# SSD chunk states of a hybrid decoder trunk: from two fp32 products in the block of y to six fp32r products inside the next projection unit

## What is computed

```python
def step(h, inp):                      # one chunk of 128 tokens
    xc, dtc, bc, cc = inp
    cum = jnp.cumsum(dtc * a, axis=1)
    ...
    y = jnp.einsum('btsg,btsgh,bsghp->btghp', scores, decay, xdt)
    y = y + jnp.einsum('btgn,bghpn->btghp', cc, h) * jnp.exp(cum)[..., None]
    last = cum[:, -1]
    w_end = jnp.exp(last[:, None] - cum)
    h_new = h * jnp.exp(last)[..., None, None] + jnp.einsum('bsgn,bsgh,bsghp->bghpn', bc, w_end, xdt)
    return h_new, y
```

## Time and profile before

| what | value |
|---|---|
| median of 3 runs | 950.2 us (949.51 to 950.45) |
| the profiled execution's own time | 950.12 us |
| its span, first to last instruction | 947.5 us |
| PE busy | 936.0 us (99%), mean granted clock 0.999 |
| DVE busy | 683.9 us (72%) |
| ACT busy | 426.2 us (45%) |
| POOL busy | 43.5 us (5%) |
| DMA | 112.54 MB, mean 119 GB/s |

### The profile page before, as it was taken

One profiled execution on the slowest core, in us unless ns is written; L12 is line 12 of the kernel. 1 busy time (PEld: TensorE's weight loads), 2 busy tenths in 40 slices (PEclk: granted clock), 3 DMA queues, 4 the chain that ended last, 5 costly groups with the idle time before them and its releaser, 6 DMA issues.

```text
span 947.5 us, 18763 instructions
## 1 busy us (share of the span) xinstructions
PE 936.0 (99%) x7928; PEld 890.6 (94%) x7928; DVE 683.9 (72%) x934; ACT 426.2 (45%) x714; POOL 43.5 (5%) x148
## 2 busy tenths in 40 slices
PE   9999999999999999999999999999999999999996
PEld 7999999999989889999999999999999988999996
DVE  6897778766986569674558877778689757786544
ACT  6432553325774145533343225532377643555243
POOL 0000101110010000000000001111101000000000
PEclk9999999999999999999999999999999999999999
DMA  7334212144335463423432342122423451652222
GB/s 279 106 125 134 69 67 67 53 127 141 109 90 174 139 230 126 141 80 114 133 128 72 131 145 68 46 68 69 161 90 122 134 194 61 225 204 73 87 71 100
DMA packets 38420, 112.54 MB, mean 119 GB/s; under 512 B 11104, under 2 KB 14048, under 8 KB 36928
## 3 DMA queue, kind: packets, MB, share of 16 engines
q1 hardware_dynamic: 37936, 109.87, 35.5%
q0 software_dynamic: 256, 0.88, 0.3%
q10 hardware_dynamic: 144, 0.59, 0.2%
HBM read 93.85 MB, written 17.47 MB: 118 GB/s over the span
## 4 chain that ended last, share of the span: by engine, by line
PE 90%; DVE 4%; ACT 4%; issue 1%; DMA 0%; SPq 0%; DVEq 0%; ACTq 0%
PE acc L564 26%; PE acc L566 25%; PE acc L565 25%; PE misc L709 1%; ACT decay L1054 1%; PE misc L695 1%; PE misc L762 1%; ACT w_hi L962 1%; PE misc L784 1%; DVE w_lo L1250 1%; PE acc L854 1%; PE misc L803 1%; PE misc L834 1%; ACT decay L1061 1%; PE misc L726 1%; DVE conv_out L1613 1%
## 5 line engine op out<-in xcount | busy, mean ns | idle before, releaser
L564 PE MATMUL acc<-hin,w_hi 128*128 128x288 f32 x1504 | 450.9, 300 | 0.3 <-DVE x L1698 0.3
L566 PE MATMUL acc<-hin,w_lo 128*128 128x288 f32 x1504 | 442.9, 295 | 0.0
L565 PE MATMUL acc<-hin,w_hi 128*128 128x288 f32 x1504 | 442.9, 294 | 0.0
L564 PEld LDWEIGHTS acc<-hin,w_hi 128*128 128x128 f32 x1504 | 282.1, 188 | 13.0 <-issue 11.3
L962 ACT ACTIVATE w_hi<-w_raw 128x1024 fp32r<-128x1024 f32 x119 | 125.7, 1056 | 366.4 <-PE acc L566 365.8
L565 PEld LDWEIGHTS acc<-hin,w_hi 128*128 128x128 f32 x1504 | 282.3, 188 | 0.4
L566 PEld LDWEIGHTS acc<-hin,w_lo 128*128 128x128 f32 x1504 | 282.1, 188 | 0.0
L1250 DVE TENSOR_TENSOR w_lo<-w_raw,w_hi 128x1024 fp32r<-128x1024 f32 x119 | 145.4, 1222 | 118.7 <-ACT w_hi L962 118.3
L564 PE MATMUL acc<-mix,w_hi 128*128 128x288 f32 x416 | 123.4, 297 | 0.7 <-DVE vT L1277 0.4
L566 PE MATMUL acc<-mix,w_lo 128*128 128x288 f32 x416 | 122.5, 295 | 0.0
L565 PE MATMUL acc<-mix,w_hi 128*128 128x288 f32 x416 | 122.5, 294 | 0.0
(11 more groups left out here) (226 smaller groups left out, 1053.5 us busy)
## 6 DMA issues: line engine op xcount, KB each, us to landing
w_raw<-in_w SPq DMA_DIRECT2D x119, 512.0 KB, 3.6
decay<-cum_rows SPq DMA_DIRECT2D x8, 1024.0 KB, 7.1
h<-in_ssm SPq DMA_DIRECT2D x16, 512.0 KB, 6.2
out_ssm_s<-h SPq DMA_DIRECT2D x16, 512.0 KB, 6.0
x<-in_x SPq DMA_DIRECT2D x7, 576.0 KB, 7.1
x_kept<-x SPq DMA_DIRECT2D x4, 576.0 KB, 3.0
x<-x_kept SPq DMA_DIRECT2D x4, 576.0 KB, 6.1
out_y<-x SPq DMA_DIRECT2D x8, 288.0 KB, 2.4
```

The costliest lines, as they stand in the source:

```text
L564: pe.matmul(out, wh, hi, start=k == 0, stop=False)
L565: pe.matmul(out, wh, lo, start=False, stop=False)
L566: return pe.matmul(out, wl, hi, start=False, stop=k == KT - 1)
```

## The change

It makes these edits:

- The two fp32 state sums leave `ssd_y`. A new `ssd_states(t)` makes six fp32r products of 512 columns (for each group high B by high `xdw`, high B by low `xdw`, low B by high `xdw`). It is called inside `project` of the next even unit, 28 + 2t, behind its fifth step of sixteen, and waits for `s_xlo`.
- ACT writes the copy of B as fp32r (the high part). After reading an even unit's result it waits for `s_xdt` and copies `xdw` to fp32r, 128x1024 (signals `s_xhi`).
- DVE subtracts for the low part of B (128x256, ahead of `ssd_weights`) and for the low part of `xdw` (128x1024, a new `ssd_low`, behind `ssd_weights` and ahead of `pool`; it waits for `s_xhi`, signals `s_xlo`, and writes over `xdw`).
- `ssd_2` keeps the multiplication of the state (now signalled as `s_elu`, for which ACT's `el` waits in place of `s_h`) and the additions of y. The addition of the sum moves to a new `ssd_state`, at the end of DVE's odd turn, behind `c_decay`; it signals `s_h`.
- In unit 34 `pool_mm_` runs as the second insert, behind step 8, as before.

`ssd_turn` is not edited: it still waits for `s_h` and `s_y`.

```diff
+        xdw_lo = place("xdt_to_end_low", [P, HEADS * HD], F32R, at=work + 4 * 7168)
+        xdw_hi = place("xdt_to_end_high", [P, HEADS * HD], F32R, at=two_at)
+        btok_2 = place("b_tok_high_low", [P, 2, GROUPS * P], F32R, at=masked)
@@ PE
+            def ssd_states(t):
+
+                pe.wait_ge(*of(s_xlo, t + 1))
+                for g in range(GROUPS):
+                    b, c = slice(g * P, (g + 1) * P), slice(g * 512, (g + 1) * 512)
+                    pe.matmul(mb[:, g, :], btok_2[:, 0, b], xdw_hi[:, c], start=True, stop=False)
+                    pe.matmul(mb[:, g, :], btok_2[:, 0, b], xdw_lo[:, c], start=False, stop=False)
+                    mm = pe.matmul(mb[:, g, :], btok_2[:, 1, b], xdw_hi[:, c], start=False, stop=True)
+                mm.then_inc(s_S, 1)
+
             def ssd_y(t):
                 n = rows(t)
                 pe.wait_ge(*of(s_xdt, t + 1))
                 pe.wait_ge(*of(s_bt, t + 1))
-                if t < TILES - 1:
-                    for g in range(GROUPS):
-                        mm = pe.matmul(mb[:, g, :], btok[:, g, :], xdw[:, g * 512:(g + 1) * 512], start=True, stop=True)
-                    mm.then_inc(s_S, 1)
                 pe.wait_ge(*of(s_M, t + 1))
@@
-                    elif U_GPOOL < u < U_GPOOL + 4 and (u - S_SSD) % 2 == 0:
-                        project(u, lambda: pool_mm_(u - U_GPOOL - 1))
+                    elif S_SSD < u < S_SST and (u - S_SSD) % 2 == 0:
+                        sums = functools.partial(ssd_states, (u - S_SSD) // 2 - 1)
+                        if U_GPOOL < u < U_GPOOL + 4:
+                            project(u, sums, 4, functools.partial(pool_mm_, u - U_GPOOL - 1), KT - 1)
+                        else:
+                            project(u, sums, 4)
@@ ACT
                     if t > 1:
-                        eng.wait_ge(*of(s_h, t))
+                        eng.wait_ge(*of(s_elu, t - 1))
                     go(act(el[:, :], m[:, :, CH - 1], ACT.Exp), s_row, t)
@@
-                        go(act(btok[:, :, :], mb[:, 3, 0:256].rearrange("p (g n) -> p g n", g=2), ACT.Copy),
-                           s_bt, t + 1)
+                        if t < TILES - 1:
+                            go(act(btok_2[:, 0, :], mb[:, 3, 0:256], ACT.Copy), s_bt, t + 1)
+                        else:
+                            go(act(btok[:, :, :], mb[:, 3, 0:256].rearrange("p (g n) -> p g n", g=2), ACT.Copy),
+                               s_bt, t + 1)
@@
+                    if even and t < TILES - 1:
+                        eng.wait_ge(*of(s_xdt, t + 1))
+                        go(act(xdw_hi[:, :], xdw[:, :], ACT.Copy), s_xhi, t + 1)
@@ DVE
+            def ssd_low(t):
+
+                eng.wait_ge(*of(s_xhi, t + 1))
+                settle()
+                go(V.tensor_tensor(xdw_lo[:, :], xdw[:, :], xdw_hi[:, :].bitcast(F32), ALU.subtract), s_xlo, t + 1)
+
             def ssd_weights(t):
                 n = rows(t)
+                if t < TILES - 1:
+                    eng.wait_ge(*of(s_bt, t + 1))
+                    go(V.tensor_tensor(btok_2[:, 1, :], mb[:, 3, 0:256], btok_2[:, 0, :].bitcast(F32), ALU.subtract))
                 eng.wait_ge(*of(s_exp, t + 1))
@@
+            def ssd_state(t):
+
+                eng.wait_ge(*of(s_S, t + 1))
+                st = mb[:, 0:2, :].rearrange("p a n -> p (a n)")
+                if t == 0:
+                    eng.wait_ge(*of(rp_out, 32))
+                settle()
+                if t == 0:
+                    go(V.tensor_copy(hT[:, :], st), s_h, 1)
+                else:
+                    go(V.tensor_tensor(hT[:, :], hT[:, :], st, ALU.add), s_h, t + 1)
+
             def ssd_2(t):
                 n = rows(t)
-                if t < TILES - 1:
-                    eng.wait_ge(*of(s_S, t + 1))
...
-                        go(V.tensor_tensor(hT[:, :], hT[:, :], st, ALU.add), s_h, t + 1)
-                    settle()
-                eng.wait_ge(*of(s_Y, t + 1))
+                eng.wait_ge(*of(s_Y, t + 1))
+                if 0 < t < TILES - 1:
+                    settle()
+                    go(V.tensor_tensor(heads(hT[:, :]), heads(hT[:, :]),
+                                       el[:, :].unsqueeze(2).to_broadcast([P, HEADS, HD]), ALU.mult), s_elu, t)
+                settle()
                 for j in range(PAIRS):
@@
                         (ssd_weights if even else ssd_2)(t)
+                        if even and t < TILES - 1:
+                            ssd_low(t)
                         if (u - S_SSD) % 2 == 1 and t + 1 < TILES - 1:
                             c_decay(t + 1)
+                        if not even and t < TILES - 1:
+                            ssd_state(t)
```

More of the change, by code:

```diff
@@ L2 @@
 from contextlib import ExitStack
+import functools
 import numpy as np
@@ L319, in trunk @@
         s_bt = sem("ssd_b_tok", TILES)
+        s_elu = sem("ssd_decay_used", TILES - 2)
+        s_xhi = sem("ssd_to_end_high", TILES - 1)
+        s_xlo = sem("ssd_to_end_split", TILES - 1)
         s_exp = sem("ssd_exps", TILES)
@@ L1433, in c_decay @@
                         go(ins, s_ec, t)
+            def ssd_state(t):
[8 more added lines that the diff above has]
+                    go(V.tensor_tensor(hT[:, :], hT[:, :], st, ALU.add), s_h, t + 1)
             def ssd_2(t):
                 n = rows(t)
-                if t < TILES - 1:
-                    eng.wait_ge(*of(s_S, t + 1))
-                    st = mb[:, 0:2, :].rearrange("p a n -> p (a n)")
-                    if t == 0:
-                        eng.wait_ge(*of(rp_out, 32))
-                        settle()
-                        go(V.tensor_copy(hT[:, :], st), s_h, 1)
-                    else:
-                        eng.wait_ge(*of(s_Y, t + 1))
[L1446 to L1449, removed]
-                        go(V.tensor_tensor(hT[:, :], hT[:, :], st, ALU.add), s_h, t + 1)
+                eng.wait_ge(*of(s_Y, t + 1))
+                if 0 < t < TILES - 1:
                     settle()
-                eng.wait_ge(*of(s_Y, t + 1))
+                    go(V.tensor_tensor(heads(hT[:, :]), heads(hT[:, :]),
+                                       el[:, :].unsqueeze(2).to_broadcast([P, HEADS, HD]), ALU.mult), s_elu, t)
+                settle()
                 for j in range(PAIRS):
```

## The result

The changed kernel takes 965.42 us (median of 4 runs, 963.59 to 966.45) against 950.12 us before: a ratio of 1.0162, 95% interval 1.015 to 1.0174. It is slower by 15.3 us, and stays inside the range of 958.5 to 967. The profiled execution took 963.59 us, with a span of 961.7.

What follows compares the result with a forecast made beforehand. PE, busy 99%, was taken as the bound. Per layer, waits of 8.20 us less 0.20 and 1.84 of work gave +6.16, +12.3 in all: 950.12 to 962.4 us, range 958.5 to 967.

Steps and rivals of the forecast that it cites:

- The bound and the mechanism: PE's issued work sets the time; with s_h last in DVE's odd turn, PE's next turn must wait for it.
- The sum: Per layer: waits 8.20, less 0.20, less 1.84 of PE work, giving +6.16; +12.3 in all, 962.4 us.
- DVE's chain in chunk 1: Units 28, 29: low part of xdw from 241.65, state multiplication at 248.38, addition done 255.55, PE's turn at 255.63.
- y's waits: PE waits for s_M before y, no longer covered by the state sum: 0.52, 0.67, 0.54 us in chunks 0 to 2.
- chunk 3: Units 32 to 34: no new waits; pooling product 0.20 earlier, products save 0.46, shift +6.16.
- The price of the products: Six fp32r products of 512 columns take 1.35 us in place of 1.81, saving PE 0.46 a chunk.
- The turn's waits: PE waits for DVE's state addition at the turns after chunks 1 and 2: 3.09 and 3.38 us.
- Rival 3: PE's clock falls in each layer's two long waits, about 2.1 us a fall: 966.6 or 970.8 us; chance 0.08.
- my signs of being wrong: Turns of units 30 and 32 start without wait, six products cost 1.8 or more, or granted clock leaves 1.00 there.
- SP: State store and four loads, waiting for chunk 3's s_h, start about 0.8 us later against PE; hidden.
- Rival 1: The change does what its work count says and is faster: -4.0 us, about 946.2; chance 0.03.
- Rival 2: Only y's waits appear, because DVE hides more: -0.6 us, 949.5, no measurable change; chance 0.03.

Runs made afterwards that it cites:

- run 1: The changed kernel with DVE's addition of the state ahead of c_decay instead of behind it: 954.4 us, ratio 1.0047 against the kernel before.
- run 3: The kernel before, fp32 sums kept in the block of y, with only the state's addition moved behind y's additions and c_decay: 955.81 us, ratio 1.0067.
- Run 4: The changed kernel with 18 idle fp32r products of 288 columns on PE ahead of the turns of units 30 and 32: 962.02 us, ratio 1.0128.
- run 9: The kernel of run 5 with DVE's low part of xdw moved behind the pooling group: 947.41 us, ratio 0.9976 against the kernel before.
- run 5: The changed kernel with the addition ahead of c_decay, pooling groups moved to unit 30 and turn 34, and s_M signalled in halves: 947.95 us, ratio 0.9981.
- run 2: The changed kernel with the fourth pooling group (5.1 us of DVE) moved from unit 30 to unit 32: 967.38 us, ratio 1.0197.
- run 6: The changed kernel with only the pooling groups moved, third to unit 30, fourth to turn 34 behind the second gate: 957.8 us, ratio 1.0084.
- run 7: The changed kernel with only s_M signalled in halves, for each group of heads: 967.23 us, ratio 1.0181.
- run 8: The changed kernel with the sums behind the unit's ninth step instead of the fifth (pooling product behind the tenth): 967.14 us, ratio 1.018.

## Why the prediction was right, point by point

**The bound and the mechanism: right.** "The change makes `s_h` the last thing of that turn" is what runs 1 and 3 show from both sides.

**The sum: right to 0.2 us a layer, without the clock.** I had +6.16 a layer. Run 4, where the clock stayed up, has 86.31 - 79.99 = +6.32 (86.31 is the mean of its two layers). Its 962.02 us stand beside the forecast of 962.4. DVE's chain in chunk 1 came within 0.1 us from the low part of `xdw` on: multiplication 248.38 forecast, 248.36 measured; turn 255.63 and 255.66. PE's own errors, on y's waits and on the products, are larger than that. They leave the sum alone in chunks 1 and 2, because DVE sets the turn there and PE's wait takes up the difference. In chunk 3 two errors offset each other, which is luck: the pooling product came 0.31 nearer to the product before it, not 0.20, and the six products saved 0.32 and not 0.46 (21.55 - 22.19 = -0.64 in run 4, beside -0.66).

**The price of the products: the saving was mis-sized.** Six products took 1.35 in my sum. The timeline of PE after:

```profile
226.84 0.40 PE L701 MATMUL misc<-xdt_to_end_high,b_tok_high_low 128*128 128x512 f32 x1
227.07 0.39 PE L702 MATMUL misc<-xdt_to_end_low,b_tok_high_low 128*128 128x512 f32 x1
...
227.99 0.39 PE L703 MATMUL misc<-xdt_to_end_high,b_tok_high_low 128*128 128x512 f32 x1
228.22 0.29 PE L571 MATMUL acc<-hin,w_hi 128*128 128x288 f32 x1
```

228.22 - 226.84 = 1.38, and 1.40 in six of the eight chunks: at the upper end that I had from the width. By the Trainium skill ("TensorE: Matmul & The Clock Gate", Back-to-back issue gap), which gives its formula for a single product's gap and not for a stream with weight loads, the estimate was 1.30 for six; the measurement decides against it, 0.23 a product instead of 0.216.

The other half of the term was wrong too. The four passes of the old sum took 0.43 each, 1.72 in all; the 1.81 held 0.09 more, which I had put down to the change of the kind of product for the lower bound and then took as saved. The rows of the kernel before place it elsewhere:

```profile
241.58 0.59 PE L695 MATMUL misc<-xdt_to_end,b_tok 128*128 128x512 f32 x1
242.10 0.34 PE L709 MATMUL misc<-decay,xdt 128*64 128x128 f32 x2
```

The last pass is followed after 0.52 and not 0.43, and both sides of this step are fp32. The step from fp32r to fp32 is 240.16 to 240.29, the normal 0.13. So the 0.09 belongs to the start of y, and it is still paid: in run 9, y follows the last fp32r product after 0.22 (240.21 to 240.43) where 0.13 is normal. The gain is 1.72 - 1.38 = 0.34 a chunk (0.32 with 1.40), and not 0.46, as the 0.35 and 0.33 of run 9's chunks 0 and 1 say too. Inside the changed kernel this error hardly shows, because in chunks 1 and 2 DVE sets the turn.

**y's waits: right.** 0.52, 0.67 and 0.54 were forecast for chunks 0 to 2. In run 4's first layer the brackets plus 0.16 of overlap give 0.61, 0.83 and 0.72, each about 0.1 to 0.2 more. The hand-over from DVE to PE, which I set at 0.08, explains it: 0.15 us (222.61 to 222.76) and twice 0.26 (240.98 to 241.24, 263.98 to 264.24) in that layer.

**The turn's waits: right in kind, a little high.** Forecast 3.09 and 3.38. Measured 2.81 at 255.66. At 279.28 it was 2.45, because PE came 1.3 us later there: it had lost time to the clock before, and DVE's chain, which sets the turn, hardly had (279.28 against a forecast of 278.95; 279.00 in run 4).

**Rival 3, the clock: it came in part, and I had it too low.** I gave 0.08 to any fall. The mean granted clock of the changed kernel is 0.992 to 0.994 in its four runs and 0.997 or 0.998 in the four of run 4, so falls are its rule. The two executions at 0.992 took 966.3 and 966.5 us, the two at 0.994 963.6 and 964.6. Run 4 puts the falls at 3.0 to 3.4 us of the 15.3. That the granted clock leaves 1.00 in these units was also one of my signs of being wrong, and it came true. The step that failed was the comparison with the 5 us that PE idles at the kernel's end at full clock: I took that stretch as what a wait must reach, and shorter ones were enough. The price of a fall was too high: 2.1 us forecast, while the two of the profiled execution cost 0.17 and 1.44 (86.47 and 87.76 beside 86.30 and 86.32). By what the Trainium skill says (same page, The HAM clock gate) the idle state is the throttled one; the traces here agree that an idle PE can come back at 0.50, also inside the work. The time still fell inside the range, since that range reached to 967 for this case. The central 962.4 was met by run 4, in which the clock stayed up; the 3 us above it are this rival's.

**SP: right.** The store and the loads of the sample states are issued at 296.92 and 297.31 in the kernel after, 7.4 us later than before, of which PE's own shift is 6.5. No wait for them is in PE's list.

**Rivals 1 and 2** had conditions that runs 5 and 9 bring about by other edits: only then does the change of products pay. The kernel as changed met neither.

## What to carry to other kernels

An engine that is 72% busy can be full where it counts. Before a signal is moved to the end of an engine's turn, write down when that turn ends now and when the waiter arrives: here 253.56 against 252.27 told the sign before anything else did. Work that is removed from the bounding engine may have been the cover for another engine's lateness (y's waits), so look at what stood behind it; and when moving work to a place where an engine idles, look at what is queued behind that place (run 2). If a wait of the bounding engine can't be avoided, its price can be more than its length: here the clock behind four such waits cost some 3 us on top.

## What the runs showed of the hardware

- PE's granted clock fell to 0.50 towards the end of, or up to 1.5 us behind, 14 of the 18 waits of 2.3 to 3.7 us by the brackets (the profiled executions of the changed kernel and of runs 2, 6, 7 and 8). It fell behind none of the waits of 0.6 to 1.7 us in runs 1, 3 and 4. Equal waits behaved differently: 2.64 us in unit 30's turn brought a fall in the changed kernel and none in run 8.
- A fall doesn't always cost what it takes from PE. In the first layer of the changed kernel it fell into the stretch where DVE set the next turn, and the layer is 0.17 us longer than in run 4 (86.47 and 86.30). In the second layer it came behind the last such wait, and the layer is 1.44 longer (87.76 and 86.32).
- An fp32r product of 512 columns takes 0.230 to 0.233 us in a stream (six in 1.38 to 1.40), one of 288 columns 0.1325 (the projection's products). By the width alone it would be 0.236, so the price lies just below a multiple of the width, and above half of an fp32 pass (0.215).
- The step from fp32r to fp32 products costs PE nothing here (240.16 to 240.29 before, 286.83 to 286.96 in run 4: 0.13 as inside the stream). The first product of y, with weights of 64 columns, starts 0.09 late behind either kind (0.52 instead of 0.43, and 0.22 instead of 0.13 in run 9). Its weight load starts with it at 242.10, where the sum's first weight load started 0.13 ahead. Whether the width of the weights or the waits in front of y cause this, no run separates.
- DVE's subtraction that writes fp32r from 128x1024 takes 1.22 us in the kernel after (1.21 to 1.23 in the rows read), and the one of 128x256 out of PSUM 0.41, as in the rows that I had taken for them.
